# Expert weights in whole slabs of 4 MiB over a ring of four slots, instead of 2 MiB parts over nine places

## What is computed

```python
logits = (xt @ w_router).astype(jnp.float32) + b_router.astype(jnp.float32)
top_v, top_i = lax.top_k(logits, TOP_K)                 # 4 of 32 experts for each token
gates = jax.nn.softmax(top_v, axis=-1)
...
def expert_block(args):
    xb, e = args
    hdn = xb @ w_gate_up[e] + b_gate_up[e]              # 1024 -> 2048
    return clamped_swiglu(hdn) @ w_down[e] + b_down[e]  # 1024 -> 1024
...
x = x + gt_f[:, None, :] * rms_norm(y, g_post_ffn[l])
# second block: x + 0.5 * swiglu(...), a Fourier and attention mixer, x + 0.5 * swiglu(...)
```

## Time and profile before

| | us |
|---|---|
| median of 3 runs | 1748.58 |
| lowest, highest | 1745.88, 1753.21 |
| the profiled execution's own time | 1747.47 |
| its span in the profile | 1745.3 |

### The profile page before, as it was taken

One profiled execution on the slowest core, in us unless ns is written; L12 is line 12 of the kernel. 1 busy time (PEld: TensorE's weight loads), 2 busy tenths in 40 slices (PEclk: granted clock), 3 DMA queues, 4 the chain that ended last, 5 costly groups with the idle time before them and its releaser, 6 DMA issues. The chain is left out here.

```text
span 1745.3 us, 26090 instructions
## 1 busy us (share of the span) xinstructions
PE 1471.5 (84%) x10135; PEld 843.9 (48%) x10135; DVE 740.6 (42%) x1420; ACT 454.2 (26%) x872; POOL 24.4 (1%) x48
## 2 busy tenths in 40 slices
PE   3998888887798998669977666659999999999998
PEld 1985622222232333113322111128888778878887
DVE  4645523323233233313322221336774546457664
ACT  2434400000010000000100000026554536255553
POOL 2001000000000000000000000000000000000000
PEclk9999899999899999989998888879999999999999
DMA  9855889999999999999999999972465731155460
GB/s 351 324 205 198 358 352 426 426 424 426 425 425 427 426 415 409 425 425 428 424 426 425 425 425 428 425 284 98 170 228 198 277 132 49 51 203 193 147 259 28
DMA packets 69013, 549.33 MB, mean 315 GB/s; under 512 B 6001, under 2 KB 6778, under 8 KB 44250
## 3 DMA queue, kind: packets, MB, share of 16 engines
q1 hardware_dynamic: 66392, 542.67, 75.6%
q0 software_dynamic: 1744, 3.53, 0.7%
q10 hardware_dynamic: 690, 0.48, 0.1%
HBM read 545.59 MB, written 1.07 MB: 313 GB/s over the span
## 5 line engine op out<-in xcount | busy, mean ns | idle before, releaser
L1307 PE MATMUL PS<-ring,arena 128*32 128x512 f32 x2768 | 345.9, 639 | 95.2 <-DMA ring<-in_w_gate_up 91.3
L1032 PE MATMUL PS<-ht_pair,weights_high 128*128 128x512 f32 x832 | 296.8, 400 | 3.5 <-DVE ht_pair L1568 2.0
L1580 DVE TENSOR_TENSOR weights_low<-ring,weights_high 128x1024 fp32r<-128x1024 f32 x204 | 248.0, 1220 | 110.5 <-ACT weights_high L709 110.5
L1949 DVE TENSOR_SCALAR arena<-PS 128x256 f32<-128x256 f32 x47 | 19.9, 424 | 530.2 <-PE PS L1307 530.2
L1307 PEld LDWEIGHTS PS<-ring,arena 128*32 128x32 f32 x2768 | 84.2, 113 | 324.9 <-issue 185.4
L709 ACT ACTIVATE weights_high<-ring 128x1024 fp32r<-128x1024 f32 x204 | 214.2, 1056 | 92.2 <-PE PS L1028 92.1
L1034 PE MATMUL PS<-ht_pair,weights_low 128*128 128x256 f32 x832 | 235.2, 283 | 0.0
L709 ACT ACTIVATE arena<-PS 128x256 f32<-128x256 f32 (+2 forms) x237 | 100.6, 432 | 516.6 <-PE PS L1364 340.0
L1032 PEld LDWEIGHTS PS<-ht_pair,weights_high 128*128 128x128 f32 x832 | 158.4, 190 | 41.6 <-issue 4.6
L709 ACT ACTIVATE arena<-arena 128x256 f32<-128x256 f32 (+2 forms) x113 | 45.7, 405 | 461.8 <-DVE arena L1949 456.9
L1034 PEld LDWEIGHTS PS<-ht_pair,weights_low 128*128 128x128 f32 x832 | 159.7, 192 | 0.0
(11 more groups left out here) (273 smaller groups left out, 1561.0 us busy)
## 6 DMA issues: line engine op xcount, KB each, us to landing
ring<-in_w_gate_up SPq DMA_DIRECT2D x117, 2048.0 KB, 34.7
ring<-in_w_down SPq DMA_DIRECT2D x54, 2048.0 KB, 36.1
ring<-in_w_ada SPq DMA_DIRECT2D x6, 4096.0 KB, 16.1
ring<-in_w_in SPq DMA_DIRECT2D x6, 4096.0 KB, 13.2
arena<-in_w_gate_up SPq DMA_DIRECT2D x11, 2048.0 KB, 36.2
arena<-in_w_down SPq DMA_DIRECT2D x10, 2048.0 KB, 36.9
ring<-in_ffn_wg SPq DMA_DIRECT2D x4, 4096.0 KB, 13.4
ring<-in_ffn_wu SPq DMA_DIRECT2D x4, 4096.0 KB, 18.9
```

The source lines that it names most:

```text
L1032: mm(PS[:, bank, :].rearrange("p (a t) -> p a t", a=2), high, HT_PAIR[:, :, k, :], start=first, stop=False, skip_group_check=True)
L1307: ins = mm(PS[CH * t:CH * (t + 1), c % INL, :].rearrange("p (u n) -> p u n", u=2), XTE[b][c % INL][:, KT // 2 * half + k, :], w[:, k % 2, ...
L1580: v.tensor_tensor(low, w, high, ALU.subtract).then_inc(sem("split_low"), 1)
```

## The change

The ninth place goes; two neighbouring parts become one transfer of 4 MiB into a whole slot. The 96 slabs of the experts go over slots 2, 0, 1, 3 in this order. A slab waits until both halves of the slab four before it have been used, or, in the first round, for the slot's last user. Both halves of a slab are announced by one semaphore, so PE's wait for the first half is for the whole slab. The dense slabs after the experts take slots 3 and 2 in turn, not 2 and 3. What PE, DVE and ACT compute, and the order of it, stay.

```diff
-PARTS = 9
-PLACES = (0, 1, 2, 4, 5, 6, 7, 3, 8)
+PARTS = 8
+PLACES = (4, 5, 0, 1, 2, 3, 6, 7)
...
-                slot = 2 + turn % 2
+                slot = 3 - turn % 2
                 turn += 1
...
         def part_at(place):
 
-            return ring[:, PART * place:PART * (place + 1)] if place < 2 * SLOTS else area(3072, PART)
+            return ring[:, PART * place:PART * (place + 1)]
 
         def part_use(u):
 
             place = PLACES[u % PARTS]
-            return place, 16 * (u // PARTS + 1 + (pre_uses[place // 2] if place % 2 == 0 and place < 2 * SLOTS else 0))
+            return place, 16 * (u // PARTS + 1 + pre_uses[place // 2])
...
-        part_full = [slot_full[h // 2] if h % 2 == 0 and h < 2 * SLOTS else sem(f"part{h}_full") for h in range(PARTS)]
+        part_full = [slot_full[h // 2] for h in range(PARTS)]
...
-            def load_part(u):
-                place = part_use(u)[0]
-                if u >= PARTS:
-                    v = u - PARTS
-                    sp.wait_ge(part_mm[v % 6], done(v // 6))
-                elif place in (0, 1):
+            def load_parts(u):
+
+                e, j, place = u // 6, u % 6, part_use(u)[0]
+                if u >= PARTS:
+                    for v in (u - PARTS, u + 1 - PARTS):
+                        sp.wait_ge(part_mm[v % 6], done(v // 6))
+                elif place == 0:
                     sp.wait_ge(*release[ADA[-1]])
-                elif place in (2, 3):
+                elif place == 2:
                     sp.wait_ge(*release[WOUT])
-                elif place in (4, 5):
+                elif place == 4:
                     sp.wait_ge(*release[ADA[-2]])
-                elif place in (6, 7):
-                    sp.wait_ge(sem("piece_mm"), wo1_done)
                 else:
-                    sp.wait_ge(sem("biased"), 1)
-                sp.dma_start(*expert_part(u % 6, u // 6, place)).then_inc(part_full[place], 16)
+                    sp.wait_ge(sem("piece_mm"), wo1_done)
+                slab = ring[:, PART * place:PART * place + SLAB]
+                if j < 4:
+                    w = a["w_gate_up"][0, e].rearrange("(p k) n -> p k n", p=P)[:, 2 * j:2 * j + 4, :]
+                    dst = slab.rearrange("p (k n) -> p k n", k=KT // 2)
+                else:
+                    w = a["w_down"][0, e].rearrange("(p k) n -> p k n", p=P)
+                    dst = slab.rearrange("p (k n) -> p k n", k=KT)
+                sp.dma_start(dst, w).then_inc(part_full[place], 16)
...
-            for u in range(6 * NE):
-                load_part(u)
+            for u in range(0, 6 * NE, 2):
+                load_parts(u)
```

More of the change, by code:

```diff
@@ L529, in _ @@
         def _(sp):
-            def expert_part(j, e, place):
-                if j < 4:
[L533 to L536, removed]
-            def load_part(u):
-                place = part_use(u)[0]
-                if u >= PARTS:
-                    v = u - PARTS
-                    sp.wait_ge(part_mm[v % 6], done(v // 6))
-                elif place in (0, 1):
-                    sp.wait_ge(*release[ADA[-1]])
-                elif place in (2, 3):
-                    sp.wait_ge(*release[WOUT])
-                elif place in (4, 5):
-                    sp.wait_ge(*release[ADA[-2]])
-                elif place in (6, 7):
-                    sp.wait_ge(sem("piece_mm"), wo1_done)
-                else:
-                    sp.wait_ge(sem("biased"), 1)
-                sp.dma_start(*expert_part(u % 6, u // 6, place)).then_inc(part_full[place], 16)
+            def load_parts(u):
[4 more added lines that the diff above has]
+                elif place == 0:
+                    sp.wait_ge(*release[ADA[-1]])
+                elif place == 2:
+                    sp.wait_ge(*release[WOUT])
+                elif place == 4:
+                    sp.wait_ge(*release[ADA[-2]])
+                else:
+                    sp.wait_ge(sem("piece_mm"), wo1_done)
+                slab = ring[:, PART * place:PART * place + SLAB]
+                if j < 4:
+                    w = a["w_gate_up"][0, e].rearrange("(p k) n -> p k n", p=P)[:, 2 * j:2 * j + 4, :]
+                    dst = slab.rearrange("p (k n) -> p k n", k=KT // 2)
+                else:
+                    w = a["w_down"][0, e].rearrange("(p k) n -> p k n", p=P)
+                    dst = slab.rearrange("p (k n) -> p k n", k=KT)
+                sp.dma_start(dst, w).then_inc(part_full[place], 16)
             def load(g):
```

## The result

The changed kernel takes 1755.43 us (median of 20 runs, 1750.08 to 1760.09) against 1747.64 us for the kernel before (20 runs, 1741.38 to 1753.21). The ratio is 1.0043, 95% interval 1.0031 to 1.0055: about 7.5 us slower, less than the 0.5% named in the prediction and clearly more than nothing. Its profiled execution has a span of 1754.9 us.

What follows compares the result with a forecast made beforehand. The expert stage lasts as long as its 402.65 MB of weights take to arrive over busy DMA engines. Terms +5.0 - 6.6 + 2.4 + 2.4 + 1.8 = +5.0 us take the median from 1748.58 to 1753.6; range 1743 to 1763.

Steps and rivals of the forecast that it cites:

- Cost of a byte: Expert weight stream: 32 KB packets in half the number, at 8.6 ns a packet, save 6.6 us.
- Start: Start of the expert stream: without the ninth place, slab 4 finds an empty queue; +5 us (3 to 7).
- Middle: Mid-stage, near 676 us: slab 48 is issued too late and the queue runs dry; +2.4 us (0 to 6).
- Elsewhere I find the reserve of three slabs longer than PE's lag: Rest of the expert stage: three queued slabs, 29 us, outlast PE's lag, so no further dry spell.
- A share under 1.00 at other places: Sign of being wrong: DMA share under 1.00 at places other than the forecast dry spells.
- PE waited less for weights: Sign of being wrong: PE waiting less than before for weights in the stretch from 700 us on.
- End: End of the expert stage: PE waits for whole slabs and gets 32 matmuls at once; +2.4 us beyond the other terms.
- FF1's wait: Next feed-forward's first gate slab is issued only after the last down product; +1.8 us (1.2 to 2.7).
- (a): Weight stream: packets stay at 16 KB or longer ones are no cheaper; +11.6, so 1760 us; chance 0.15.
- (b): Ring too coarse: four slots run dry longer where PE falls behind; 8 us more, 1762; chance 0.13.
- (c): Faster: 20 ns a packet, no dry middle, warm tail; 1740 us; chance 0.08.
- (d): Queued transfers did pay the skill's fixed price for each transfer; some 190 us faster; chance 0.01.

Runs made afterwards that it cites:

- pairs_together: Changed kernel with each slab sent as two 2 MiB transfers, PE still waiting for both halves before starting on it; ratio 1.0102 against the kernel before.
- packets_8k: Kernel before with each 2 MiB part sent as two 1 MiB transfers in 8 KB runs; ratio 1.0069.
- eight_places: Kernel before with its ninth place taken away: 2 MiB parts over eight places in plain order, each issued and awaited by itself; ratio 1.0044.
- pairs_apart: Changed kernel with each slab sent as two 2 MiB transfers, PE waiting for each half separately, places given back in pairs; ratio 1.0060 against the kernel before.
- best_slabs: Changed kernel with dense slab order turned back, the arena's place used once for half of slab 4, and the last slab in two separately awaited halves; ratio 1.0051.
- last_in_parts: Changed kernel with dense slab order turned back and expert 31 alone in six 2 MiB parts, each awaited by itself; ratio 1.0008 against the kernel before.
- ninth_once: Changed kernel with the arena's place used a single time, for the first half of slab 4; ratio 1.0038 against the kernel before.
- changed_again: The changed kernel run once more, unaltered; ratio 1.0031 against the kernel before.
- late_slabs: Kernel before up to expert 17, then whole 4 MiB slabs over four slots in experts 18 to 30, then expert 31 in parts; ratio 0.9994.
- hybrid: As best_slabs without the single arena use, but every fourth slab goes as two parts round slot 2's halves and the arena's place; ratio 1.0020.

## Why the prediction was right, and where its steps were off

It forecast +5.0 us (1753.6 from 1748.6, a ratio of 1.0029); +7.5 was measured, inside its range and in the direction that it gave.

The mechanisms were the right ones; nearly every term was set too low, and a gain that no term names made up for part of it.

- **Cost of a byte: right.** 32 KB packets in half the number, and 8.6 ns each: 6.3 us between pairs_together and the changed kernel for a term of 6.6, and 13.2 for 13.2 in packets_8k. It counted along the whole stream, in front of the dry spell at 678 us (3.1 of the 6.3, 6.6 of the 13.2) as behind it, because the experts that run into it had waited for weights themselves and start earlier with them.
- **Start: right in place, short in size.** +5 was forecast; slab 8 came 7.5 us late, 0.7 of it because the stage began that much later in this execution (SP issued slab 4 at 234.15, not 233.4). The price of the empty queue was too low: 12.1 us for a slab, measured 13.2 (slab 4). eight_places reproduces 5.2 of the 7.5 by the missing place alone; the rest comes with the larger unit.
- **Middle: right in place, incomplete.** The dry spell stands at 678 us where it was put at 676. It is a term of its own, as forecast: behind slab 47 or part 95 the lateness grows by 2.8 us in the changed kernel (+4.7 to +7.5), and by 2.3 to 3.0 in the other runs that give places back as whole slabs throughout, pairs_apart aside (0.7), however late they run. "Elsewhere I find the reserve of three slabs longer than PE's lag" was wrong: at 646 us slab 45 was issued on a nearly empty queue (share 0.58), which cost 1.2 us, and 850 to 860 has 0.90. A share under 1.00 at other places was one of the prediction's own signs of being wrong. Another came too: PE waited less for weights in 700 to 1130 us (72.7 us against 78.8).
- **Start and middle together** were 7.4 us in the forecast. With 16 KB packets (pairs_together) they come to 10.6 at part 97, so they were 3.2 too low. The packets took 3.1 off that by slab 48 and 3.2 behind it.
- **A gain without a term.** From part 97 to the end pairs_together needed 473.5 us and the kernel before 475.3, so 1.8 us come back with no long packet: 10.6 - 6.3 - 1.8 = 2.5, the measured lateness of the last landing (forecast 0.8). The cause is open. A trace of it is in the completion marks, of which each transfer leaves sixteen, one for each DMA engine: in the kernel before the last mark of a part is 5.1 us behind the mean of its sixteen at part 97 and 14.7 at part 191; in the changed kernel 1.5 and 8.5, in pairs_together 1.6 and 7.9. So the slowest engine falls back less in these two. That the dry spells let it draw level fits this, but was not tried.
- **End: right in sign and path.** Forecast 2.4, measured 3.1 (5.8 us from last landing to the end of the down product instead of 2.7). The working had the path through the last gate and up slab and its 32 matmuls, between 3.6 and 7.3 us; 6.6 came, where about 6 was taken. Only its heading names the wrong slab: splitting the last slab leaves 5.6 us (best_slabs), splitting the last expert leaves 2.0 (last_in_parts). The size varies between executions: the same slabs left 4.1 us in ninth_once, where the 32 matmuls took 4.9.
- **FF1's wait: right, mis-sized.** 1.8 forecast, 2.6 measured twice, since the load took 13.9 us where 13.2 was put in.
- **Rivals.** (a), packets that stay at 16 KB or are no cheaper, is refuted. (b), a ring too coarse, came in part: the larger unit costs 5.8 us at the end of the down product (pairs_together against eight_places), spread over the start, the middle and the end, not 8 more in the middle. (c) asked for 20 ns a packet, which packets_8k excludes. (d) is refuted by pairs_together: 96 more transfers cost what their packets cost. The Trainium skill gives the fit that (d) starts from ("DMA: Bandwidth & Descriptors", "Anatomy of one DMA") for transfers that GpSimd issues, and the rule quoted beside it speaks of overlap with compute; the transfers here are issued by SP and overlap one another.

At the last down product the forecast was +5.0 with FF1's wait, and 5.6 + 2.6 = 8.2 us were measured. That the total came within 2.5 us of the measured 7.5 owes something to luck: start, middle, end and FF1 were together 4.7 us too low and the packet gain 0.3 too high, and 1.8 us came back for a reason that the prediction does not have. No experiment priced the 1.4 us behind the split; changed_again makes it a difference between executions.

## What to carry to other kernels

Longer packets were worth 8 to 9 ns a packet in a full queue, so look first at what the larger unit costs. Here one place of nine taken away cost 4.6 us at the end of the last product, as large a ratio as the whole change, and giving places back in pairs and waiting for whole slabs cost 5.8 more; 768 fewer packets in each engine did not pay for both. Price the two apart, by a run with the small unit on fewer places and one with the small transfers tied in pairs. In this stream PE mostly waits for weights and is behind only now and then, and both a late start (late_slabs) and a cheaper byte (pairs_together against the changed kernel) were carried through to the end, so that such terms add up. What did not carry was one extra place used once (ninth_once). And when a ring's order is turned, read which slot is freed last: the first load of the next stage must not stand behind it.

## What was new about the hardware

- A filled queue lands 4 MiB each 9.71 us in 32 KB packets, and in the stretch of 300 to 600 us it moved 428 GB/s, against 426 at 16 KB and 419 at 8 KB.
- PE's 32 matmuls of a chunk take 3.64 us right behind other work. When PE had stood for 3.3 to 4.9 us before them they took 6.3 to 6.6 us in the changed kernel and best_slabs, 4.9 and 5.2 in ninth_once and hybrid, and 6.4 and 5.0 in pairs_together. The granted clock of such stretches is lower: 0.66 in 1140 to 1160 us of the changed kernel.

```profile
1140.00:1160.00 20.00, 13.31 (x66) 2.94 (x66) 0.94 (x3) 0.51 (x2) 0.00 (x0) 0.66 0.61 261
```

- In that same stretch the DMA share is 0.61 though the last slab lands only at 1161.8. Its sixteen completion marks lie at 1148.3 to 1149.1 (seven), 1155.5 to 1157.3 (eight) and 1161.8 (one). Those of part 191 in the kernel before lie at 1137.0 to 1137.8 (seven), 1148.1 to 1149.6 (eight) and 1159.3 (one), while those of part 17 all lie within 1.8 us. PE waits for the last one, so the end of the stream was set by the slowest of the sixteen engines, 9.7 us behind the next one before and 4.5 us in the changed kernel. Why it is behind was not tried.
